# Last expert sums in the PSUM banks, norm weight as one row, and a square moved: a change to a hybrid decoder step with 32 experts

## The chip, the cores and the metric

One core of a Trainium2 chip. The metric is the device time of one launch in microseconds (us); the figure of the kernel before is the median of three runs. All data are f32.

## The reference

One decoder layer serves 256 prompt tokens (one sequence) and 8 sample tokens (eight sequences, one new token each) with the same weights, D = 1024. Adaptive norm, two recurrent mixers (HGRN2 and GLA), output projection and residual, a second norm, then a mixture of 32 experts of which each token takes 4, and a last norm. What matters here is the end:

```
h  = rms_norm(x, norm2_g) * (1 + sc2) + sh2
for each token, the sum over its 4 experts of
     gate * ( act(h @ w_up[e] + b_up[e]) @ w_down[e] + b_down[e] )
x  = x + g2 * that sum
y  = x * rsqrt(mean(x * x) + 1e-6) * final_norm_g
```

The weights are w_up (32, 1024, 2048) and w_down (32, 1024, 1024), 12 MB for an expert and 403 MB for all; every expert is read once.

## The kernel before, in words

The program is written for each engine by itself, with semaphores between them; nothing plans or reorders. SP issues the weight loads from HBM into SBUF as pieces of 2 MB (`pairs`, a ring of eight), in the order in which TensorE uses them, and waits before a piece until the one that had its place is used. A turn n of the expert loop (generator `experts`: four turns written out, hardware loops, four written out from `MIDDLE_AT` = 16 on, a loop, two written out) does on TensorE, in this order: gather of the tokens of expert n+1 by a one-hot product (line 1402), transposes of the up product (`back`, line 1449), `turn`, `combine` of expert n-1, first half of the up product of n+1 (`up`, line 1431), `gates` (line 1460), both halves of the down product of n (`down`, line 1486), and the second half of the up product. 64 slots serve an expert: 8 sample tokens and up to 56 prompt tokens; if an expert has more, an overflow loop at the end (`n_over > 0`) works through the rest.

`down` leaves the result of an expert as 128 partitions by 512: half 0 of the columns in partitions 0 to 63, half 1 in 64 to 127. VectorE multiplies it with g2 into `ysb` (`take_rows`, line 2097), and adds the sample rows to `acc_s` (line 2108). `combine` (line 1472) spreads `ysb` back to the tokens with the gates as the stationary operand: four products of 64 rows by 512 columns, for the blocks (0,0), (0,1), (1,0), (1,1) of the 256 x 1024 result (`COMBINE`), into four PSUM banks (`SUM_BANKS`, for the last two experts `LAST_BANKS` = 4, 7, 6, 0). VectorE adds the four banks to `acc` in SBUF (`add_up`, line 2092), which began as the residual x.

In turn 16, `biases` on TensorE and VectorE adds the experts' down biases of all tokens at once, and ends with two sets of sample rows (`rows`, line 1277) that ScalarE copies out of bank 4 (line 923, `take_sample_rows`): x and g2 of the samples. TensorE waits for both copies before it goes on with the gates.

At the end TensorE does: `back` of expert 31, down of 30 (two pieces of 16 instructions), down of 31 first half, combine of 30, down of 31 second half, combine of 31. Then the last norm:

- VectorE adds block by block (line 2092). ScalarE squares blocks 0, 1, 2 out of `acc` with an accumulator (line 962), VectorE the fourth (line 2202) and adds the partial sums (line 2206).
- ScalarE makes the reciprocal root (lines 968, 969). VectorE makes block (1,0) times weight (line 2208), ScalarE scales it (line 973); VectorE does the other three blocks in one instruction each (line 2212).
- The samples: GpSimd puts `ys` together (lines 661, 662, 664) and multiplies it with the weight (line 666); ScalarE squares it with an accumulator (line 971), TensorE adds the halves (line 1630), ScalarE takes root (lines 975, 976) and scales (line 978).
- SP writes four blocks of 256 KB (line 582) and two sample halves (line 585), each waiting for its own block, in the order (0,0), (0,1), (1,0), (1,1), samples.

The norm weight `fgrow`, the same row in all 128 partitions, and `fgs`, its halves in partitions 0 to 63 and 64 to 127, come by DMAs that repeat the row (lines 562 and 564), issued when the last up product is done.

Of the kernel before, what the change touches and what calls it, by code (L numbers as in the profile page):

```python
# [21 lines left out]
ALU = mybir.AluOpType  # L22
ACT = mybir.ActivationFunctionType
AX = mybir.AxisListType

P = 128
D = 1024
# [5 lines left out]
NE = 32  # L33
# [19 lines left out]
XE = 1  # L53
# [206 lines left out]
def build_step(nc, a, o):  # L260
    ctx = ExitStack()
    with ctx:
# [111 lines left out]
        fgrow = more[:, 0, :]  # L374
        fgs = more[:, 1, 0:512]
        bd = r_x[:, 512:1024]
        bdg = r_s[:, 1536:2048]
# [79 lines left out]
        def _(sp):  # L457
# [86 lines left out]
            for i in range(UPS):  # L544
                reuse(i)
                load(i, 0, "up", i)
            for e, e0, q in experts(sp):
                body(e, UPS + LOADS * e0, q)
            for e, kind, k in LAST[:-1]:
# [41 lines left out]
        def _(pool):  # L591
# [72 lines left out]
            od.link(g.tensor_tensor(ys, ys, junk_s, ALU.add), sem("ys_ready"))  # L664
            pool.wait_ge(sem("fg_in"), 48)
            od.did(g.tensor_tensor(yfs, ys, fgs, ALU.mult), sem("yfs_ready"))
# [3 lines left out]
        def _(act):  # L670
# [275 lines left out]
            with act.If(n_over > 0):  # L946
                with act.Fori(0, EXTRA) as j:
                    with act.If(j < n_over):
                        n = j + NE
                        take_gathered(n)  # L950
                        take_up(n)
                        take_gates(n)
                        glu_sigmoid(n, j * 2 + 2 * NE, n + 1)
                        act.nop()
                    act.nop()
                act.wait_ge(sem("acc_done"), 1)
# [27 lines left out]
        def _(pe):  # L984
# [477 lines left out]

            def combine(n, banks, xes, sampled=None, picks=None, gT=gpickT):

# [4 lines left out]
                for (i, half), b in zip(COMBINE, banks):  # L1469
                    if b == 6:  # L1470
                        pe.wait_ge(sem("xe_ready"), xes * XE)
                    mm(bank[:, b, :], gT[64 * half:64 * half + 64, P * i:P * i + P],  # L1472
                       ysb[64 * half:64 * half + 64, :], start=True, stop=True).then_inc(sem("acc_psum"), 1)

# [54 lines left out]
            def biases(n):  # L1529
# [80 lines left out]
            with pe.If(n_over > 0):  # L1610
                with pe.Fori(0, EXTRA) as j:
                    with pe.If(j < n_over):
# [11 lines left out]
                        pe.nop()  # L1624
                    pe.nop()
                pe.nop()

            pe.wait_ge(sem("pair_ready"), 4)
            pe.wait_ge(sem("squares_ready"), 4)
            mm(bank[:, 2, 0:1], pair[:, :], sumsq_s[:, :], start=True, stop=True).then_inc(sem("ssq_psum"), 1)  # L1630
# [3 lines left out]
        def _(dve):  # L1634
# [541 lines left out]
            with dve.If(n_over > 0):  # L2176
                with dve.Fori(0, EXTRA) as j:
                    with dve.If(j < n_over):
# [18 lines left out]
                    dve.nop()  # L2197
                v.memset(sumsq[:, 4:5], 0.0).then_inc(sem("acc_done"), 1)
                dve.nop()

            dve.wait_ge(sem("acc_used"), NA * NE)
            STT(ring[:, 15, 0:512], acc[1][:, 512:D], 1.0, acc[1][:, 512:D], ALU.mult, ALU.mult, accum_out=sumsq[:, 3:4]
                ).then_inc(sem("sums_ready"), 1)
            dve.wait_ge(sem("sums_ready"), 1)
            dve.wait_ge(sem("squares_ready"), 3)
            TT(sumsq[:, 5:7], sumsq[:, 0:4:2], sumsq[:, 1:4:2], ALU.add).then_inc(sem("sums_ready"), 1)
            dve.wait_ge(sem("fg_in"), 48)
            TT(ring[:, 13, 0:512], acc[1][:, 0:512], fgrow[:, 0:512], ALU.mult).then_inc(sem("yf1_ready"), 1)
            dve.wait_ge(sem("frstd_ready"), 1)
            for i, half in ((0, 0), (0, 1), (1, 1)):  # L2210
                own = slice(512 * half, 512 * half + 512)
                STT(ring[:, 12 + i, own], acc[i][:, own], sumsq[:, 5 + i:6 + i], fgrow[:, own], ALU.mult, ALU.mult
                    ).then_inc(sem("y0_ready"), 1)

# [67 lines left out]
```

## Time and profile before

| | us |
|---|---|
| median of 3 runs | 1158.92 (1158.68 to 1160.07) |
| the profiled execution, its own time | 1159.39 |
| its span, first to last instruction | 1157.6 |
| mean granted TensorE clock | 0.994 |
| TensorE (PE) busy | 1112.3 |
| VectorE (DVE) busy | 411.7 |
| ScalarE (ACT) busy | 191.3 |
| GpSimd (POOL) busy | 20.7 |
| read from HBM | 455.60 MB, 398 GB/s over the span |

PE is TensorE's matmuls and PEld its weight loads, which run beside them. A matmul of f32 shows as two instructions. SPq and the like are the sequencers' own work, such as issuing a DMA. An engine's busy time is no measure of what it costs: what counts is who waits for whom. The granted clock is a share of 2.4 GHz. Rows with "xN" merge N instructions that follow one another; the time beside them is from the first start to the last end.

### The profile page before, as it was taken

What the parts mean: (1) busy time and instruction counts of PE and PEld (TensorE: products, weight loads), DVE (VectorE), ACT (ScalarE), POOL (GpSimd) and SP (SyncE); (2) the same over time, 40 slices, a digit from 0 to 9 for tenths busy, and PEclk for the clock granted to TensorE, in tenths of its full rate; (3) what the DMA queues carried; (4) which work ended last, traced back from release to release, by engine and by line L of the source; (5) the groups of instructions that cost most, each with busy time, mean ns of one, the idle gap of its engine ahead of it and who ended that gap; (6) DMA issues with size and microseconds to landing.
All of it is one profiled execution on the core that took longest, in us unless ns stands there. A gap on an engine that the chain in (4) does not pass through costs nothing.

```text
span 1157.6 us, 14316 instructions
## 1 busy us (share of the span) xinstructions
PE 1112.3 (96%) x5674; PEld 497.2 (43%) x5674; DVE 411.7 (36%) x841; ACT 191.3 (17%) x387; POOL 20.7 (2%) x53
## 2 busy tenths in 40 slices
PE   7999999999999999999999998999999999999996
PEld 5777778843333333333333333333333333333332
DVE  3145644353333333333333334333333333333334
ACT  2161223321111111111111111111111111111112
POOL 0101010000000000000000000000000000000001
PEclk9999999999999999999999998999999999999998
DMA  9987986989999999999999999999999999999995
GB/s 352 411 308 257 367 274 231 415 316 400 429 412 430 429 426 427 429 428 428 429 429 429 429 429 427 428 427 427 427 430 425 428 428 429 428 429 428 428 429 199
DMA packets 43323, 460.96 MB, mean 398 GB/s; under 512 B 6965, under 2 KB 7937, under 8 KB 13673
## 3 DMA queue, kind: packets, MB, share of 16 engines
q1 hardware_dynamic: 37072, 449.66, 93.2%
q0 software_dynamic: 2688, 9.47, 2.3%
q10 hardware_dynamic: 3512, 1.14, 0.4%
q8 instruction: 34, 0.56, 0.2%
q14 instruction: 17, 0.13, 0.0%
HBM read 455.60 MB, written 4.65 MB: 398 GB/s over the span
## 4 chain that ended last, share of the span: by engine, by line
PE 73%; DMA 25%; DVE 1%; ACT 1%; issue 0%; SPq 0%; DVEq 0%; ACTq 0%
PE bank L1431 27%; DMA ring<-in_w_up 20%; PE bank L1486 14%; PE bank L1091 9%; PE bank L1472 5%; PE bank L1402 4%; DMA ring<-in_w_down 3%; PE bank L1314 2%; PE bank L1449 2%; DMA ring<-in_w_ada 2%; PE bank L1036 1%; PE bank L1411 1%; PE bank L1195 1%; PE bank L1460 1%; PE bank L1172 1%; PE bank L1277 1%
## 5 line engine op out<-in xcount | busy, mean ns | idle before, releaser
L1431 PE MATMUL bank<-ring,arena 128*64 128x512 f32 x2016 | 448.6, 595 | 21.2 <-DMA ring<-in_w_up 21.2
L1431 PEld LDWEIGHTS bank<-ring,arena 128*64 128x64 f32 x2016 | 139.7, 137 | 320.2 <-issue 277.0
L1486 PE MATMUL bank<-ring,arena 128*64 128x512 f32 x992 | 220.1, 595 | 1.9 <-DMA ring<-in_w_down 1.9
L1486 PEld LDWEIGHTS bank<-ring,arena 128*64 128x64 f32 x992 | 68.6, 137 | 131.8 <-issue 129.0
L1091 PE MATMUL bank<-arena,ring 128*128 128x264 f32 x448 | 105.4, 390 | 0.8 <-DVE arena L1696 0.8
L2043 DVE COPY arena<-bank 128x512 f32<-128x512 f32 x32 | 22.1, 692 | 197.9 <-PE bank L1431 197.9
L890 ACT ACTIVATE arena<-bank 128x512 f32<-128x512 f32 x32 | 19.1, 598 | 442.1 <-PE bank L1431 442.1
L1091 PEld LDWEIGHTS bank<-arena,ring 128*128 128x128 f32 x448 | 83.1, 190 | 17.9 <-issue 4.5
L2097 DVE TENSOR_TENSOR arena<-bank,arena 128x512 f32<-128x512 f32 x32 | 22.1, 692 | 189.7 <-PE bank L1486 189.7
L2092 DVE TENSOR_TENSOR arena<-arena,bank 128x512 f32<-128x512 f32 x128 | 79.1, 680 | 5.4 <-PE bank L1472 5.4
L1472 PE MATMUL bank<-arena,gpickT 64*128 64x512 f32 x248 | 78.6, 628 | 0.0
L2052 DVE TENSOR_TENSOR arena<-bank,bupT 128x512 f32<-128x512 f32 x64 | 43.9, 686 | 70.6 <-PE bank L1449 70.6
L1402 PE MATMUL bank<-arena,before 128*64 128x512 f32 x256 | 60.4, 592 | 0.0
L1975 DVE TENSOR_TENSOR arena<-before,arena 128x256 f32<-128x256 f32 x32 | 13.6, 425 | 119.4 <-PE bank L1460 119.3
L905 ACT ACTIVATE gpickT<-bank 128x256 f32<-128x256 f32 x31 | 11.9, 385 | 215.8 <-PE bank L1460 215.8
L1449 PEld LDWEIGHTS bank<-ident,arena 128*128 128x128 f32 x256 | 33.2, 209 | 25.0 <-issue 24.3
L1472 PEld LDWEIGHTS bank<-arena,gpickT 64*128 64x128 f32 x248 | 29.8, 185 | 27.6 <-issue 15.6
L1449 PE MATMUL bank<-ident,arena 128*128 128x128 f32 x256 | 39.1, 296 | 0.5 <-ACT arena L890 0.5
L1402 PEld LDWEIGHTS bank<-arena,before 128*64 128x64 f32 x256 | 18.3, 137 | 36.1 <-issue 36.0
L896 ACT ACTIVATE arena<-arena 128x512 f32<-128x512 f32 x32 | 20.1, 630 | 57.5 <-DVE arena L2057 57.5
L1314 PE MATMUL bank<-arena,ring 128*128 128x264 f32 x128 | 29.2, 388 | 0.0
L1314 PEld LDWEIGHTS bank<-arena,ring 128*128 128x128 f32 x128 | 24.1, 190 | 5.0 <-issue 1.1
(335 smaller groups left out, 688.4 us busy)
## 6 DMA issues: line engine op xcount, KB each, us to landing
ring<-in_w_up SPq DMA_DIRECT2D x125, 2048.0 KB, 29.1
ring<-in_w_down SPq DMA_DIRECT2D x61, 2048.0 KB, 28.1
ring<-in_w_ada SPq DMA_DIRECT2D x24, 1024.0 KB, 9.5
ring<-in_w_in SPq DMA_DIRECT2D x14, 1024.0 KB, 12.0
ring<-in_w_o SPq DMA_DIRECT2D x4, 1024.0 KB, 8.5
arena<-in_w_up SPq DMA_DIRECT2D x5, 512.0 KB, 18.8
arena<-in_w_down SPq DMA_DIRECT2D x5, 512.0 KB, 12.8
ring<-in_state_hgrn POOLq DMA_DIRECT2D x4, 512.0 KB, 13.3
```

Source lines behind the costliest of these rows:

```text
L896: act.activation(te, tg, ACT.Exp, scale=-ALPHA).then_inc(sem("glu_step"), 1)
L1091: last = mm(bank[:, proj_bank(n), 0:T], ring[:, slot, 512 * (k % 4) + P * i:512 * (k % 4) + P * i + P], hT[:, k, :], start=(k == 0), stop= ...
L1314: last = mm(bank[:, WO_BANK[m % 3], 0:T], ring[:, FRONT_SLOT[ld], c0:c0 + P], oT[:, k, :], start=(k == 0), stop=(k == KT - 1))
L1402: last = mm(bank[64 * half:64 * half + 64, 6, :], pick[:, i, :], h2tok[:, i, 512 * half:512 * half + 512], start=(i == 0), stop=(i == 1))
L1431: last = mm(bank[64 * half:64 * half + 64, b, :], xe[:, par, k % 4, k // 4, :], src[:, 512 * half:512 * half + 512], start=(k == 0), stop= ...
L1449: last = tr(bank[:, 2 + b, P * j:P * j + P], us[:, c0:c0 + 4 * P - 3:4], ident[:, :])
L1472: mm(bank[:, b, :], gT[64 * half:64 * half + 64, P * i:P * i + P], ysb[64 * half:64 * half + 64, :], start=True, stop=True).then_inc(sem(" ...
L1486: last = mm(bank[64 * half:64 * half + 64, b, :], acts[:, k, :], src[:, 512 * half:512 * half + 512], start=(k == 0), stop=(k == KT - 1))
L2043: v.tensor_copy(us[:, 512:1024], bank[:, 1, :]).then_inc(sem("us_dve"), 1)
L2052: return TT(dst.rearrange("p (j h s) -> p j h s", j=4, h=2), bank[:, 2 + b, :].rearrange("p (j h s) -> p j h s", j=4, h=2), bias(b).to_bro ...
L2092: TT(y, y, bank[:, b, :], ALU.add).then_inc(sem("acc_used"), 1)
L2097: TT(ysb, bank[:, b, :], g2h, ALU.mult).then_inc(sem("ysb_ready"), 1)
```

## The change

Six things change.

1. Before the first down product of expert 31, TensorE multiplies the identity with the four blocks of `acc`, into the four last banks, and leaves the sums open (`sums_to_banks(False)`).
2. The combines of experts 30 and 31 accumulate onto these banks (`start=False`). VectorE's eight adds of these experts go, and so does TensorE's wait for the adds of 30. If the overflow loop runs, VectorE first copies the banks back to `acc`, and TensorE puts the sums into the banks again at the end.
3. The last norm reads the banks in place of `acc`. ScalarE squares blocks 0, 2 and 3; VectorE copies block 1 to SBUF and squares it from there and from the bank.
4. The square of the samples goes from ScalarE to VectorE, ahead of the addition of the partial sums.
5. `final_norm_g` is loaded as one row into one partition, before the loads of turn 16; the three repeating DMAs at the end go.
6. In turn 16, after the sample rows, TensorE multiplies a row of ones with each half of this row, into banks 4 and 7, and ScalarE copies these into `fgrow` and `fgs`, two copies for each half; TensorE waits for all four.

```diff
@@ block.sync
             for e, e0, q in experts(sp):
+                if e0 == MIDDLE_AT:
+                    sp.wait_ge(sem("down_done"), 3)
+                    sp.dma_start(fgraw, a["final_norm_g"].unsqueeze(0)).then_inc(sem("fg_in"), 16)
                 body(e, UPS + LOADS * e0, q)
...
-            sp.wait_ge(sem("up_done"), NE)
-            sp.dma_start(fgrow, a["final_norm_g"].unsqueeze(0).to_broadcast([P, D])).then_inc(sem("fg_in"), 16)
-            for half in range(2):
-                sp.dma_start(fgs[64 * half:64 * half + 64, :], a["final_norm_g"][512 * half:512 * half + 512].unsqueeze(0)
-                             .to_broadcast([64, 512])).then_inc(sem("fg_in"), 16)
@@ block.scalar, take_sample_rows
+                for half in range(2):
+                    act.wait_ge(sem("bias_psum"), half + 6)
+                    own, b = slice(64 * half, 64 * half + 64), (4, 7)[half]
+                    act.activation(fgrow[:, 512 * half:512 * half + 512], bank[:, b, :], ACT.Copy).then_inc(sem("rows_sb"), 1)
+                    act.activation(fgs[own, :], bank[own, b, :], ACT.Copy).then_inc(sem("rows_sb"), 1)
@@ block.scalar, the end
-            def square(m):
-                i, half = COMBINE[m]
-                act.wait_ge(sem("acc_used"), NA * (NE - 1) + m + 1)
-                od.did(A(ring[:, 14, 512 * m:512 * m + 512], acc[i][:, 512 * half:512 * half + 512], ACT.Square,
+            for m in (0, 2, 3):
+                act.wait_ge(sem("acc_psum"), NA * (NE - 1) + m + 1)
+                od.did(A(ring[:, 14, 512 * m:512 * m + 512], bank[:, LAST_BANKS[m], :], ACT.Square,
                          accum_out=sumsq[:, m:m + 1]), sem("squares_ready"))
-            for m in range(3):
-                square(m)
-            act.wait_ge(sem("sums_ready"), 2)
+            act.wait_ge(sem("sums_ready"), 4)
             od.link(A(sumsq[:, 5:7], sumsq[:, 5:7], ACT.Ln, scale=1.0 / D, bias=eps_col[:, 0:1]))
             od.link(A(sumsq[:, 5:7], sumsq[:, 5:7], ACT.Exp, scale=-0.5), sem("frstd_ready"))
-            act.wait_ge(sem("ys_ready"), 1)
-            od.did(A(junk_s, ys, ACT.Square, accum_out=sumsq_s[:, 0:1]), sem("squares_ready"))
@@ block.tensor
+            def sums_to_banks(stop):
+                for m, ((i, half), b) in enumerate(zip(COMBINE, LAST_BANKS)):
+                    last = mm(bank[:, b, :], ident[:, :], acc[i][:, 512 * half:512 * half + 512], start=True, stop=stop)
+                    if stop:
+                        last.then_inc(sem("acc_done"), 1)
...
                 pe.wait_ge(sem("rows_sb"), 3)
+                pe.wait_ge(sem("fg_in"), 16)
+                for half in range(2):
+                    mm(bank[:, (4, 7)[half], :], ones[0:1, :], fgraw[:, 512 * half:512 * half + 512], start=True, stop=True
+                       ).then_inc(sem("bias_psum"), 1)
+                pe.wait_ge(sem("rows_sb"), 7)
...
             down(NE - 2, ld, rd)
             ld, rd = last_of(NE - 1, "down")
+            pe.wait_ge(sem("acc_used"), NA * (NE - 2))
+            pe.wait_ge(sem("gpick_sb"), NE)
+            pe.wait_ge(sem("xe_ready"), NE * XE)
+            sums_to_banks(False)
             down(NE - 1, ld, rd, (0,), 3, actT_last)
-            combine(NE - 2, LAST_BANKS, NE, None, NE)
+            combine(NE - 2, LAST_BANKS, NE, None, NE, start=False, stop=False)
             down(NE - 1, ld, rd, (1,), 3, actT_last)
-            pe.wait_ge(sem("acc_used"), NA * (NE - 1))
-            combine(NE - 1, LAST_BANKS, NE, None, NE, gpickT_last)
+            combine(NE - 1, LAST_BANKS, NE, None, NE, gpickT_last, start=False)
@@ block.vector
             take_rows(NE - 2)
-            add_up(NE - 2, LAST_BANKS)
+            dve.wait_ge(sem("acc_psum"), NA * (NE - 1))
             take_rows(NE - 1, sampled=False, b=3)
             STT(junk_s, bank[:, 3, :], gs[:, NE - 1:NE], g2s, ALU.mult, ALU.mult).then_inc(sem("acc_s_used"), 1)
-            add_up(NE - 1, LAST_BANKS)
...
-            dve.wait_ge(sem("acc_used"), NA * NE)
-            STT(ring[:, 15, 0:512], acc[1][:, 512:D], 1.0, acc[1][:, 512:D], ALU.mult, ALU.mult, accum_out=sumsq[:, 3:4]
-                ).then_inc(sem("sums_ready"), 1)
+            dve.wait_ge(sem("acc_psum"), NA * (NE - 1) + 2)
+            v.tensor_copy(ring[:, 15, 0:512], bank[:, LAST_BANKS[1], :]).then_inc(sem("sums_ready"), 1)
             dve.wait_ge(sem("sums_ready"), 1)
+            STT(ring[:, 15, 512:D], ring[:, 15, 0:512], 1.0, bank[:, LAST_BANKS[1], :], ALU.mult, ALU.mult,
+                accum_out=sumsq[:, 1:2]).then_inc(sem("sums_ready"), 1)
+            dve.wait_ge(sem("ys_ready"), 1)
+            STT(junk_s, ys, 1.0, ys, ALU.mult, ALU.mult, accum_out=sumsq_s[:, 0:1]).then_inc(sem("sums_ready"), 1)
+            dve.wait_ge(sem("sums_ready"), 2)
             dve.wait_ge(sem("squares_ready"), 3)
             TT(sumsq[:, 5:7], sumsq[:, 0:4:2], sumsq[:, 1:4:2], ALU.add).then_inc(sem("sums_ready"), 1)
-            dve.wait_ge(sem("fg_in"), 48)
-            TT(ring[:, 13, 0:512], acc[1][:, 0:512], fgrow[:, 0:512], ALU.mult).then_inc(sem("yf1_ready"), 1)
+            dve.wait_ge(sem("rows_sb"), 7)
+            TT(ring[:, 13, 0:512], bank[:, LAST_BANKS[2], :], fgrow[:, 0:512], ALU.mult).then_inc(sem("yf1_ready"), 1)
```

## Rows read from the trace of the kernel before

**Rows 1.** The page: DMA in 40 slices (tenths), and one group of instructions by line
```profile
DMA  9987986989999999999999999999999999999995
...
L2092 DVE TENSOR_TENSOR arena<-arena,bank 128x512 f32<-128x512 f32 x128 | 79.1, 680 | 5.4 <-PE bank L1472 5.4
```

**Rows 2.** The page: shares of the chain that ended last
```profile
PE 73%; DMA 25%; DVE 1%; ACT 1%; issue 0%; SPq 0%; DVEq 0%; ACTq 0%
```

**Rows 3.** Windows: busy PE, PEld, DVE, ACT, POOL, then PEclk, DMA share, GB/s
```profile
710.00:720.00 10.00, 7.65 (x42) 3.37 (x42) 2.15 (x4) 1.43 (x3) 0.00 (x0) 0.66 1.00 428
720.00:760.00 40.00, 40.00 (x188) 14.32 (x186) 11.05 (x20) 3.62 (x7) 0.00 (x0) 1.00 1.01 428
...
900.00:1000.00 100.00, 94.16 (x434) 34.12 (x430) 34.08 (x59) 12.90 (x22) 0.00 (x0) 1.00 1.01 428
```

**Rows 4.** Timeline, TensorE and VectorE from 1131 on: start, us, instruction [idle before]
```profile
1131.64 3.65 PE L1486 MATMUL bank<-ring,arena 128*64 128x512 f32 x16 [0.51 <-DMA ring<-in_w_down]
...
1136.65 3.65 PE L1486 MATMUL bank<-ring,arena 128*64 128x512 f32 x16 [1.36 <-DMA ring<-in_w_down]
...
1140.23 1.99 PE L1472 MATMUL bank<-arena,gpickT 64*128 64x512 f32 x8
...
1141.46 2.48 DVE L2092 TENSOR_TENSOR arena<-arena,bank 128x512 f32<-128x512 f32 x4 [4.77 <-PE bank L1472]
...
1142.15 3.65 PE L1486 MATMUL bank<-ring,arena 128*64 128x512 f32 x16
...
1145.85 0.69 DVE L2097 TENSOR_TENSOR arena<-bank,arena 128x512 f32<-128x512 f32 x1 [1.91 <-PE bank L1486]
...
1146.65 1.99 PE L1472 MATMUL bank<-arena 64*128 64x512 f32 x8 [0.84 <-issue]
```

**Rows 5.** Timeline, earlier TensorE products with a 128 by 128 tile
```profile
149.80 3.28 PE L1091 MATMUL bank<-arena,ring 128*128 128x264 f32 x14
...
188.86 1.98 PE L1113 MATMUL bank<-arena,ones 128*128 128x512 f32 x4
190.68 0.83 PE L1247 MATMUL bank<-ring 128*128 128x128 f32 x6
```

**Rows 6.** Timeline, what follows the last combination
```profile
1147.35 1.27 POOL L664 TENSOR_TENSOR arena<-arena 128x512 f32<-128x512 f32 x1 [7.90 <-DVE arena L2169]
...
1147.85 2.48 DVE L2092 TENSOR_TENSOR arena<-arena,bank 128x512 f32<-128x512 f32 x4 [0.65 <-PE bank L1472]
...
1148.70 1.27 POOL L666 TENSOR_TENSOR arena<-arena,more 128x512 f32<-128x512 f32 x1
...
1149.81 0.61 ACT L962 ACTIVATE ring<-arena 128x512 f32<-128x512 f32 x1
1150.33 0.19 ACT L962 ACTIVATION_READ_ACCUMULATOR ring<-arena 128x1 f32 x1
...
1151.10 0.16 DVE L2206 TENSOR_TENSOR sumsq<-sumsq 128x2 f32<-128x2 f32 x1
...
1151.94 2.08 DVE L2212 SCALAR_TENSOR_TENSOR ring<-arena,sumsq,more 128x512 f32<-128x512 f32 x3
...
1152.72 1.99 SPq L582 DMA_DIRECT2D out_yp<-ring  x4
...
1154.01 0.72 ACT L978 ACTIVATE arena<-arena,sumsq 128x512 f32<-128x512 f32 x1
1154.76 0.98 SPq L585 DMA_DIRECT2D out_ys<-arena  x2
```

**Rows 7.** The page: ScalarE's copy out of a bank
```profile
L890 ACT ACTIVATE arena<-bank 128x512 f32<-128x512 f32 x32 | 19.1, 598 | 442.1 <-PE bank L1431 442.1
```

**Rows 8.** Lines 562 and 564, the weight's DMAs, last rows of each answer
```profile
L564 SPq DMA_DIRECT2D more<-in_final_norm_g x2: 562/576/591, 1125.9 to 1126.5; - x2
...
DMA to landing us min/median/max: 16.0/16.8/17.6
```

**Rows 9.** Line 478, weight loads issued from 690 to 800
```profile
DMA to landing us min/median/max: 18.9/24.1/35.9
```

More of the change, by code:

```diff
@@ L375, in build_step @@
         fgs = more[:, 1, 0:512]
+        fgraw = more[0:1, 2, :]
         bd = r_x[:, 512:1024]
@@ L664, in _ @@
             od.link(g.tensor_tensor(ys, ys, junk_s, ALU.add), sem("ys_ready"))
-            pool.wait_ge(sem("fg_in"), 48)
+            pool.wait_ge(sem("rows_sb"), 7)
             od.did(g.tensor_tensor(yfs, ys, fgs, ALU.mult), sem("yfs_ready"))
@@ L955, in _ @@
                     act.nop()
-                act.wait_ge(sem("acc_done"), 1)
+                act.wait_ge(sem("acc_done"), 1 + NA)
                 act.nop()
-            def square(m):
-                i, half = COMBINE[m]
-                act.wait_ge(sem("acc_used"), NA * (NE - 1) + m + 1)
-                od.did(A(ring[:, 14, 512 * m:512 * m + 512], acc[i][:, 512 * half:512 * half + 512], ACT.Square,
+            for m in (0, 2, 3):
+                act.wait_ge(sem("acc_psum"), NA * (NE - 1) + m + 1)
+                od.did(A(ring[:, 14, 512 * m:512 * m + 512], bank[:, LAST_BANKS[m], :], ACT.Square,
                          accum_out=sumsq[:, m:m + 1]), sem("squares_ready"))
-            for m in range(3):
-                square(m)
-            act.wait_ge(sem("sums_ready"), 2)
+            act.wait_ge(sem("sums_ready"), 4)
             od.link(A(sumsq[:, 5:7], sumsq[:, 5:7], ACT.Ln, scale=1.0 / D, bias=eps_col[:, 0:1]))
             od.link(A(sumsq[:, 5:7], sumsq[:, 5:7], ACT.Exp, scale=-0.5), sem("frstd_ready"))
-            act.wait_ge(sem("ys_ready"), 1)
-            od.did(A(junk_s, ys, ACT.Square, accum_out=sumsq_s[:, 0:1]), sem("squares_ready"))
             act.wait_ge(sem("yf1_ready"), 1)
@@ L1461, in gates, with combine @@
                 last.then_inc(sem("gpick_psum"), 1)
-            def combine(n, banks, xes, sampled=None, picks=None, gT=gpickT):
+            def combine(n, banks, xes, sampled=None, picks=None, gT=gpickT, start=True, stop=True):
                 pe.wait_ge(sem("ysb_ready"), n + 1)
@@ L1472, in combine @@
                     mm(bank[:, b, :], gT[64 * half:64 * half + 64, P * i:P * i + P],
-                       ysb[64 * half:64 * half + 64, :], start=True, stop=True).then_inc(sem("acc_psum"), 1)
+                       ysb[64 * half:64 * half + 64, :], start=start, stop=stop).then_inc(sem("acc_psum"), 1)
+            def sums_to_banks(stop):
[3 more added lines that the diff above has]
+                        last.then_inc(sem("acc_done"), 1)
             def down(n, loads, rounds, pieces=range(DOWNS), b=5, acts=actT):
@@ L1625, in _ @@
                     pe.nop()
+                pe.wait_ge(sem("acc_done"), 1)
+                sums_to_banks(True)
                 pe.nop()
             pe.wait_ge(sem("pair_ready"), 4)
-            pe.wait_ge(sem("squares_ready"), 4)
+            pe.wait_ge(sem("sums_ready"), 3)
             mm(bank[:, 2, 0:1], pair[:, :], sumsq_s[:, :], start=True, stop=True).then_inc(sem("ssq_psum"), 1)
@@ L2176, in _ @@
             with dve.If(n_over > 0):
+                for m, ((i, half), b) in enumerate(zip(COMBINE, LAST_BANKS)):
+                    dve.wait_ge(sem("acc_psum"), NA * (NE - 1) + m + 1)
+                    for part in range(2):
+                        c0 = 256 * part
+                        v.tensor_copy(acc[i][:, 512 * half + c0:512 * half + c0 + 256], bank[:, b, c0:c0 + 256]
+                                      ).then_inc(sem("acc_used"), 1)
                 with dve.Fori(0, EXTRA) as j:
@@ L2198, in _ @@
                 v.memset(sumsq[:, 4:5], 0.0).then_inc(sem("acc_done"), 1)
+                dve.wait_ge(sem("acc_done"), 1 + NA)
                 dve.nop()
-            dve.wait_ge(sem("acc_used"), NA * NE)
-            STT(ring[:, 15, 0:512], acc[1][:, 512:D], 1.0, acc[1][:, 512:D], ALU.mult, ALU.mult, accum_out=sumsq[:, 3:4]
-                ).then_inc(sem("sums_ready"), 1)
+            dve.wait_ge(sem("acc_psum"), NA * (NE - 1) + 2)
+            v.tensor_copy(ring[:, 15, 0:512], bank[:, LAST_BANKS[1], :]).then_inc(sem("sums_ready"), 1)
             dve.wait_ge(sem("sums_ready"), 1)
+            STT(ring[:, 15, 512:D], ring[:, 15, 0:512], 1.0, bank[:, LAST_BANKS[1], :], ALU.mult, ALU.mult,
[3 more added lines that the diff above has]
+            dve.wait_ge(sem("sums_ready"), 2)
             dve.wait_ge(sem("squares_ready"), 3)
             TT(sumsq[:, 5:7], sumsq[:, 0:4:2], sumsq[:, 1:4:2], ALU.add).then_inc(sem("sums_ready"), 1)
-            dve.wait_ge(sem("fg_in"), 48)
-            TT(ring[:, 13, 0:512], acc[1][:, 0:512], fgrow[:, 0:512], ALU.mult).then_inc(sem("yf1_ready"), 1)
+            dve.wait_ge(sem("rows_sb"), 7)
+            TT(ring[:, 13, 0:512], bank[:, LAST_BANKS[2], :], fgrow[:, 0:512], ALU.mult).then_inc(sem("yf1_ready"), 1)
             dve.wait_ge(sem("frstd_ready"), 1)
@@ L2211, in _ @@
                 own = slice(512 * half, 512 * half + 512)
-                STT(ring[:, 12 + i, own], acc[i][:, own], sumsq[:, 5 + i:6 + i], fgrow[:, own], ALU.mult, ALU.mult
-                    ).then_inc(sem("y0_ready"), 1)
+                STT(ring[:, 12 + i, own], bank[:, LAST_BANKS[COMBINE.index((i, half))], :], sumsq[:, 5 + i:6 + i], fgrow[:, own],
+                    ALU.mult, ALU.mult).then_inc(sem("y0_ready"), 1)
 def ada_blocks(w):
```

## The prediction

> **What bounds the kernel now.** I read the page first: the DMA engines are full from the tenth of the 40 slices to the last but one, at half in the last [rows 1]. The chain that ended last gives TensorE 73% and DMA 25% [rows 2]. The reader is to see that these two take turns: a stage of 100 us has TensorE busy for 94 with the DMA share at 1.01 and 428 GB/s [rows 3]. So the transfer of 2 MB pieces is the floor of the long middle, and what TensorE does there costs only if it drains the queue. At the end it turns round. The timeline of the last 27 us [rows 4] shows TensorE waiting twice for weights, once 0.51 us before the second half of the down weights of expert 30 (1131.64) and once 1.36 us before the first half of those of expert 31 (1136.65). From there on it runs without a wait for DMA: 16 instructions of the down product, the combination of expert 30 (1140.23), 16 more (1142.15), and then the last combination at 1146.65, which waits for VectorE's product with g2 (1145.85). Call that start T. Everything behind T is a chain of vector operations: four adds, squares, reciprocal root, products, and six output DMAs that SP issues one behind another [rows 6]. The run ends 10.95 us after T, at 1157.6. So this change is judged by two things: how far T moves, and how long the chain behind T is.
>
> The profiled execution took 1159.39 us with its span of 1157.6, so 1.79 us lie around it; it is 0.47 us above the median of 1158.92. I sum on the span and add the difference to the median.
>
> **The identity products, TensorE.** Four products of a 128x128 identity with a 128x512 block of acc, each two instructions as every f32 product here: 8 instructions. They sit between the last down product of expert 30 and the first of expert 31. What they wait for is long done: VectorE works in order and has the adds of expert 29 behind it before it even starts the gated product of expert 31, and the copied gates belong to the turn before. The nearest rows for the price: the same tile and width, line 1113, puts four instructions in 188.86 to 190.68, 0.455 each; line 1091, the same tile with 264 columns, has 14 starts in 3.28 us, so (3.28 - 0.39) / 13 = 0.222 each, by 512/264 that is 0.431 [rows 5]. Eight cost 3.45 us (0.431) to 3.64 us (0.455); I take 3.45, since the second row has more instructions in a stream. The 16 instructions from 1131.64 make room after 3.58 us, as those from 1136.65 do (next group at 1140.23), so at 1135.22. The identity products then end at 1138.67 and the down product of expert 31 starts there, instead of 1136.65: the weight wait of 1.36 us covers part, 2.02 us are left over. If nothing hid it, it would be 3.45. What is late next is TensorE itself, for 3.58 + 1.92 + 3.65 us up to T. That the combinations now accumulate costs nothing: the down products accumulate already at the same pace (16 instructions in 3.58 us). The wait for the adds of expert 30 before the last combination goes; those adds ended at 1143.94 [rows 4], 2.7 us before T, so it held nobody. T moves to 1148.67, by +2.02 (bounds +1.9 to +2.25).
>
> **Behind T, ScalarE and VectorE.** Before, the first add starts at T+1.20, three more follow at 0.6 each, the sum of the last block comes at T+3.71, its read at T+4.33, the small addition (line 2206) at T+4.45 [rows 6]. The change takes out the four adds (2.48 us) and reads the banks. Banks 4 and 7 are there at T+1.20; banks 6 and 0 with the end of the eight matmuls, T+1.99. ScalarE: square of block 0 at T+1.20; block 2 waits for its bank, T+2.05; block 3 follows after 0.61, and its accumulator is read 0.52 + 0.19 later: T+3.37. That its source is a bank should not cost: a ScalarE copy out of a bank takes 598 ns, the square from SBUF 0.61 us [rows 6, 7]. VectorE: copy of bank 7 at T+1.20, 0.69 (an add from a bank is 680 ns [rows 1]); square at T+1.93; then the sample square, which waits for ys, ready when GpSimd's add ends (T+0.70+1.27 = T+1.97), so no wait: start T+1.93+0.70 = T+2.63, accumulator read at T+3.25 to T+3.33. The small addition then starts at T+3.42, when both are through, instead of T+4.45: 1.03 us earlier. As bounds I take 0.9 and 1.1: by 0.05 each the two squares may be longer than the rows that I use, and the small addition may come 0.07 earlier if the order of the semaphores is kinder.
>
> From there the order is as before: logarithm, exponent (0.84 us to the first final product), first product 0.75, first output DMA 0.78 after its start: T+5.04. The six issues take 3.02 us back to back (1152.72 to 1155.74 [rows 6]), and up to the end of the span there are 1.86 more. Does something arrive later than its issue? Block (1,0): its product on VectorE T+3.50, scaled by ScalarE T+4.25 to T+4.96, issue at T+6.0, no. Last final product T+4.26+2.08 = T+6.34, issue T+6.5, no, though by little. Samples: TensorE's sum over the halves is out by T+4.1 at a pair of instructions, ScalarE comes to it behind the (1,0) scaling at T+4.96, makes the root in at most the 0.84 of the other one and scales in 0.72: ready T+6.5, issue T+7.08. Before, the samples' scaling (1154.73) and SP's free slot (1154.76) came together, so moving the sample square to VectorE removes a second wait that would otherwise hold at T+8.1. The final products now take 0.69 from one start to the next and the adds out of banks 0.6 [rows 6], so a bank as their source adds nothing that I can see; 0.05 each would not reach SP, but for the first. The end moves by +2.02 - 1.03 = +1.0 us.
>
> **The norm weight.** Removed: the three repeating DMAs. The later two were issued at 1125.9 and 1126.5 and landed 16.0 to 17.6 us later, by 1144.1, before T and long before anyone multiplies with the weight [rows 8]. Together they moved 0.77 MB (128 rows of 4 KB and 128 of 2 KB) at the end of the queue; no output is under way then. Gain 0 to 0.5: should they have been mixed with the weights of expert 30, this would be 1.8 us of the stream, but TensorE is ready at 1131.64 - 0.51 = 1131.13 and only its 0.51 us of wait can go. I take 0, because the next piece comes 5.0 us later (1131.64 to 1136.65), the 4.9 us that 2.1 MB need at 428 GB/s and no more. Added: one row of 4 KB before the loads of expert 16's turn. SP's wait there is for the third down product, which is hundreds of us old; it is issued with loads that lie eight pieces, 39 us, ahead of TensorE, and the longest landing of that stretch is 35.9 us [rows 9], while TensorE asks for it only at the end of its bias stage, about 720. In the middle, behind the sample rows, two products of one row by 512 columns, four instructions, 1.7 us at full clock, and four ScalarE copies of 0.60 [rows 7] that follow from the first: 1.0 + 2.4 + 0.2 = 3.6 us by which TensorE falls back, 4.6 at half clock. In this stage TensorE waits on other engines several times already, busy 7.65 of 10 us with a granted clock of 0.66, yet the DMA share stays 1.00 [rows 3]. The pieces issued in 690 to 800 landed in 18.9 us at least, against 35.9 at most [rows 9]: the stage eats some 17 us of the queue's lead. 3.6 more leave over 15, where a piece alone needs 4.9. Cost 0; without that cover 3.6 to 4.6.
>
> The overflow loop does not run: 128 adds for 32 experts [rows 1], so its new instructions are only jumped over, VectorE's branch in the time between its product with g2 and T+1.20.
>
> **Sum:** +2.02 - 1.03 + 0 + 0 = +1.0 us: span 1158.6, profiled 1160.4, median 1159.9. A change of 0.2%, about 2.3 us here, is what can be told from none; this is less than half.
>
> **Rivals.**
> *Port (24%).* The sample square is new on VectorE, with both inputs in SBUF, and GpSimd multiplies ys with the weight at the same time: ready at T+2.05, 1.27 long, to T+3.32. In the rows of before no such pair overlaps: GpSimd's instructions run beside adds with one input in a bank (2.48 us for four, as always), and its last one ends at 1149.97, before VectorE's square of the last block [rows 6]. If VectorE's square has to wait until GpSimd is through, it starts at T+3.35 instead of T+2.63, and the small addition goes to T+4.1: 0.7 later. Then +1.7: 1160.6. Against it: no row; for it: none either. The Trainium skill states just this in SBUF — State Buffer, section Who interferes with whom: a VectorE instruction with two SBUF inputs contends with a GpSimd instruction that reads SBUF, through the shared read interface, and the pair is an exclusive lock. By that rule the time would be the 1160.6; no row of before can show it.
>
> *The tail's weights come earlier (12%).* The broadcasts slowed them: TensorE goes on at 1131.13, -0.5: 1159.4. For it speaks that all three were issued while the weights of experts 30 and 31 were under way in the same queue [rows 4, 8]; against it the steady distance of the pieces.
>
> *The middle is not hidden (5%), slower.* The place is expert 16's turn. If the standing lasts so long that the clock stays at half through the following down and up products (7.0 us each at full clock, twice that then), the lag grows by 4.6 + 7.0 + 7.0 = 18.6, while only 18.9 - 4.9 = 14.0 of lead are there; from there each us of lag is lost. That costs 4.6 us: 1164.5. It decides when the DMA share between 715 and 760 falls below 1. Against it: behind the present stall the clock is 1.00 again in the whole of 720 to 760 [rows 3].
>
> *The identity products hide wholly (5%).* TensorE has no second gap there; it would need their cost under 1.4 us, against 3.4 by two rows. Then only the gain stays: 1157.9.
>
> *My forecast (45%)*, and the rest (9%) for shifts of a us either way that no part explains; the three runs of before lie 1.4 us apart. Range 1158.2 to 1161.6: it takes in the forecast, port and earlier weights with the bounds of their terms, and leaves out the middle and the fully hidden case. Faster than 1156.6 is 5% (shifts on top of full hiding or of earlier weights), slower than 1161.2 is 12% (the middle 5, the upper ends of port and of the shifts 7), within 83%.
>
> **What would show it.** Eight identity matmuls from about 1135.2, 3.4 us, and no DMA wait before the down product of expert 31, which starts near 1138.7. The last combination at 1148.7. The small addition 3.4 us behind it (4.1 if the port rules), the first output DMA 5.0 behind. In the middle, DMA share 1.0 throughout and TensorE again waiting for weights before 900. I am wrong if T moves by less than 1.5 or more than 2.5, or if the span between T and the end does not shrink by 0.3 to 1.1.

## The result, and the profile after

The changed kernel takes 1161.53 us (median of 20 runs, 1159.99 to 1164.28), the kernel before in the same 20 rounds 1159.34 (1158.49 to 1161.24). The ratio is 1.0019, 95% interval 1.0013 to 1.0025: slower by 2.2 us, inside the 0.2% that I had called "no change", but twice the +1.0 us of my sum. The interval leaves out 1, so the loss is real, though small. The profiled execution has a span of 1159.5 us (1157.6 before).

The timeline of TensorE at the end of the changed kernel (start, us, instruction); line 1491 is `down`, 1476 the identity products, 1470 `combine`:

```profile
1127.65 7.21 PE L1491 MATMUL bank<-ring,arena 128*64 128x512 f32 x32
...
1134.80 3.70 PE L1476 MATMUL bank<-arena,ident 128*128 128x512 f32 x8
...
1138.43 3.65 PE L1491 MATMUL bank<-ring,arena 128*64 128x512 f32 x16
...
1142.01 1.99 PE L1470 MATMUL bank<-arena,gpickT 64*128 64x512 f32 x8
...
1143.93 3.65 PE L1491 MATMUL bank<-ring,arena 128*64 128x512 f32 x16
...
1148.45 1.99 PE L1470 MATMUL bank<-arena 64*128 64x512 f32 x8 [0.86 <-DVE arena L2112]
```

Against [rows 4]: eight instructions from 1134.80 to 1138.43, 3.63 us, and no wait for weights before expert 31's down product. T, the start of the last combination, is at 1148.45 instead of 1146.65.

Behind T, the timeline of VectorE, GpSimd, ScalarE and SP of the changed kernel, which answers to [rows 6]:

```profile
1149.61 0.60 ACT L965 ACTIVATE ring<-bank 128x512 f32<-128x512 f32 x1 [18.71 <-PE bank L1470]
1149.65 0.69 DVE L2222 COPY ring<-bank 128x512 f32<-128x512 f32 x1 [0.60 <-PE bank L1470]
...
1150.54 1.27 POOL L664 TENSOR_TENSOR arena<-arena,more 128x512 f32<-128x512 f32 x1
...
1150.98 1.36 DVE L2227 SCALAR_TENSOR_TENSOR arena<-arena 128x512 f32<-128x512 f32 x1
...
1151.53 0.20 ACT L965 ACTIVATION_READ_ACCUMULATOR ring<-bank 128x1 f32 x1
...
1152.28 0.15 DVE L2230 TENSOR_TENSOR sumsq<-sumsq 128x2 f32<-128x2 f32 x1
...
1153.11 2.07 DVE L2236 SCALAR_TENSOR_TENSOR ring<-bank,sumsq,more 128x512 f32<-128x512 f32 x3
...
1153.89 2.28 SPq L580 DMA_DIRECT2D out_yp<-ring  x4
...
1156.21 1.54 SPq L583 DMA_DIRECT2D out_ys<-arena  x2
```

Two things are to be seen. The sample square (line 2227) takes 1.36 us, while GpSimd's product with the weight (line 664) runs until 1151.81; the small addition waits for it and starts 0.55 us after ScalarE's last read has ended (1151.73). And the outputs: six issues take 3.86 us instead of 3.02, and from the first issue to the end there are 5.61 us instead of 4.88.

### The profile page after: what moved, and what is told of

Same layout as the page of the kernel before. It is cut to its first block, busy times and chain, and to the rows that moved or that the text cites. A ratio compares the mean times of both kernels' runs of the same rounds, so it can differ in the third digit from the quotient of the medians.

```text
span 1159.5 us, 14336 instructions
## 1 busy us (share of the span) xinstructions
PE 1119.1 (97%) x5686; PEld 500.0 (43%) x5686; DVE 408.5 (35%) x836; ACT 192.8 (17%) x389; POOL 20.6 (2%) x53
## 4 chain that ended last, share of the span: by engine, by line
PE 82%; DMA 16%; DVE 1%; ACT 1%; issue 0%; ACTq 0%; DVEq 0%; SPq 0%
PE bank L1429 31%; PE bank L1491 17%; DMA ring<-in_w_up 15%; PE bank L1089 9%; PE bank L1470 6%; PE bank L1400 4%; PE bank L1447 3%; PE bank L1312 2%; PE bank L1034 1%; PE bank L1409 1%; PE bank L1193 1%; PE bank L1458 1%; PE bank L1015 1%; DMA ring<-in_gn_gla 1%; PE bank L1170 1%; PE bank L1275 1%
## 5 line engine op out<-in xcount | busy, mean ns | idle before, releaser
L2107 DVE TENSOR_TENSOR arena<-arena,bank 128x512 f32<-128x512 f32 x120 | 74.2, 679 | 0.0
```

The source lines that it names most:

```text
L2107: TT(y, y, bank[:, b, :], ALU.add).then_inc(sem("acc_used"), 1)
```

## The experiments

All traces were read at the same points. The table's distances are in us; "first issue to end" runs from the first output DMA's issue to the end of the span, and the last column says when the last transfer of instruction code (queue 14 of the DMA view) starts, in steps of 0.2 us. T here is absolute and moves with the time at which the weights come, so the columns behind it are distances.

| kernel | T | T to small addition | T to first output issue | six issues | first issue to end | last code transfer, from first issue |
|---|---|---|---|---|---|---|
| before | 1146.65 | 4.45 | 6.07 | 3.02 | 4.88 | +0.2 |
| before, second trace | 1146.83 | 4.45 | 6.07 | 3.02 | 4.90 | +0.2 |
| e9, before with code never run | 1147.40 | 4.45 | 6.07 | 3.11 | 4.93 | +0.4 |
| e1, norm weight alone | 1147.31 | 4.45 | 6.07 | 3.15 | 4.92 | +0.4 |
| changed | 1148.45 | 3.83 | 5.44 | 3.86 | 5.61 | +0.8 |
| changed, second trace (e6) | 1148.29 | 3.84 | 5.45 | 3.86 | 5.56 | +0.8 |
| e10, without the code never run | 1148.42 | 3.85 | 5.46 | 3.87 | 5.62 | +0.8 |
| e2, new end, old norm weight | 1150.23 | 3.85 | 5.45 | 3.15 | 5.62 | +0.8 |
| e4, no identity products | 1146.43 | 3.84 | 5.45 | 3.54 | 5.32 | +0.8 |
| e3, GpSimd held back | 1148.14 | 3.39 | 5.01 | 3.03 | 5.35 | +3.0 |
| e8, identity products early | 1151.32 | 3.38 | 5.00 | 3.02 | 5.48 | +3.0 |
| e5, sample square on ScalarE | 1149.20 | 3.39 | 5.01 | 2.97 | 5.49 | +1.8 |
| e7, hybrid | 1147.20 | 4.34 | 5.96 | 3.03 | 5.74 | +3.8 |
| e11, hybrid, second version | 1147.40 | 3.58 | 5.20 | 3.03 | 5.50 | +3.2 |

**e1, the norm weight alone** (kernel before, with parts 5 and 6 of the change):

```diff
+                    sp.dma_start(fgraw, a["final_norm_g"].unsqueeze(0)).then_inc(sem("fg_in"), 16)
...
+                pe.wait_ge(sem("rows_sb"), 7)
```

> Only the weight of the last norm is changed (one row, spread by TensorE in turn 16); the end is that of before. Theory A (all of the loss lies in the tail: identity products, port, output issues): the time of before, ratio 1.000, DMA share 1.0 through 700 to 760, last combination at the same distance behind the last weight wait as before. Rival B (the middle stage costs about 1.2 us that the sum left out): ratio 1.001.

Ratio 1.0002 (0.9993 to 1.0011): the middle is hidden. The windows of the changed kernel say how (busy PE, PEld, DVE, ACT, POOL, PEclk, DMA share, GB/s), against [rows 3]:

```profile
710.00:720.00 10.00, 7.75 (x40) 3.29 (x38) 2.06 (x4) 1.15 (x2) 0.00 (x0) 0.66 1.02 433
720.00:730.00 10.00, 8.60 (x24) 2.77 (x26) 0.72 (x2) 2.69 (x6) 0.00 (x0) 0.66 1.01 429
730.00:760.00 30.00, 30.00 (x144) 10.89 (x140) 9.21 (x16) 3.47 (x6) 0.00 (x0) 1.00 1.01 427
```

and the landing of the weight loads issued from 690 to 800 in it, against [rows 9]:

```profile
DMA to landing us min/median/max: 12.6/17.3/35.4
```

The granted clock is 0.66 in 720 to 730 too (1.00 before), the DMA share never falls, and the shortest landing goes from 18.9 to 12.6 us. My 3.6 to 4.6 us of lag were 6.3, still covered, since one piece alone needs 4.9.

**e2, the new end alone** (the changed kernel with the three repeating DMAs of before):

```diff
+            sp.dma_start(fgrow, a["final_norm_g"].unsqueeze(0).to_broadcast([P, D])).then_inc(sem("fg_in"), 16)
```

> The opposite: the new end with the three repeating DMAs of before. Theory A: the time of the changed kernel, ratio 1.0019 to before. Rival B: 1.0009. If the repeating DMAs had delayed the last weights (rival of the prediction), TensorE waits for the second half of expert 30's down weights again by some 0.5 us, here as before, and it does not in the changed kernel.

Ratio 1.0020 (1.0012 to 1.0029), as the changed kernel. So the whole loss lies in the end. TensorE waited 0.51 us for the second down piece of expert 30 here, and not in the changed kernel; but the second trace of before has no such wait either, and there the three DMAs are in place. And the trace of e10 has a wait of 0.42 us at this place without the three DMAs. It comes and goes from one execution to the next. The rival of the weights that come earlier is not borne out.

**e4, no identity products** (the residual and the sums of experts 0 to 29 are left out):

```diff
-            sums_to_banks(False)
...
-            combine(NE - 2, LAST_BANKS, NE, None, NE, start=False, stop=False)
+            combine(NE - 2, LAST_BANKS, NE, None, NE, start=True, stop=False)
```

> The changed kernel without the identity products: the residual and the sums of experts 0 to 29 are left out of the result. Theory A: TensorE waits for expert 31's down weights again (about 1.4 us), the last combination comes 1.8 to 2.2 us earlier, the time falls by as much, to about 1159.5, ratio 1.0002 or a little under 1. Rival (the products are hidden by the wait for weights): no change, ratio 1.0019.

Ratio 1.0001 (0.9992 to 1.0010), against 1.0019: the identity products cost some 2.1 us, known to about 1.2 us by the two intervals. The timeline of TensorE says where:

```profile
1127.82 7.23 PE L1491 MATMUL bank<-ring,arena 128*64 128x512 f32 x32
...
1136.41 3.65 PE L1491 MATMUL bank<-ring,arena 128*64 128x512 f32 x16 [1.36 <-DMA ring<-in_w_down]
...
1146.43 1.99 PE L1470 MATMUL bank<-arena 64*128 64x512 f32 x8 [0.86 <-DVE arena L2111]
```

From the start of expert 30's down product to T it is 18.61 us, in the changed kernel 1148.45 - 1127.65 = 20.80: 2.19 more, which is 3.63 us of products less the wait of 1.36 and a little. The cost depends on the execution that one compares with. In both traces of the kernel before it is 19.17 us from there to T, with 1.87 and 1.95 us of waits for weights in them, and against these the products cost 1.63. Over the five traces without identity products (before twice, e1, e4, e9) the two waits before the down products add up to between 1.34 and 2.54 us. What should have been a gain of the new end, with the identity products taken away, still leaves nothing: the small addition is 0.61 us earlier than before, and 0.4 of it go in the outputs.

**e3, GpSimd held back:**

```diff
             pool.wait_ge(sem("rows_sb"), 7)
+            pool.wait_ge(sem("sums_ready"), 3)
             od.did(g.tensor_tensor(yfs, ys, fgs, ALU.mult), sem("yfs_ready"))
```

> The changed kernel, with GpSimd's product of ys with the weight made to wait until VectorE's sample square is done. Port theory: the sample square falls from 1.36 to 0.69 us, and the small addition comes 3.4 us behind the start of the last combination instead of 3.8; time 0.4 us less than the changed kernel. Rival (the square is long for another reason, such as both operands being one tensor): it stays 1.36 us.

The timeline of this kernel:

```profile
1150.68 0.69 DVE L2228 SCALAR_TENSOR_TENSOR arena<-arena 128x512 f32<-128x512 f32 x1
...
1151.53 0.16 DVE L2231 TENSOR_TENSOR sumsq<-sumsq 128x2 f32<-128x2 f32 x1 [0.15 <-ACT ring L966]
1151.55 1.28 POOL L665 TENSOR_TENSOR arena<-arena,more 128x512 f32<-128x512 f32 x1 [1.39 <-DVE arena L2228]
```

The same instruction, both operands still one tensor, takes 0.69 us when GpSimd is silent, and the small addition comes at T+3.39, now held by ScalarE. So it is shown that the two instructions slow VectorE's down when they run together, and that the operands being one tensor is not the reason. That it is the read interface which they share, and not for instance that both read `ys`, was not separated. Time 1161.08, ratio 1.0015 (1.0006 to 1.0023): the direction is right, the 0.4 us are below what the runs resolve.

**e5, the sample square back on ScalarE:**

```diff
-            STT(junk_s, ys, 1.0, ys, ALU.mult, ALU.mult, accum_out=sumsq_s[:, 0:1]).then_inc(sem("sums_ready"), 1)
...
+            od.did(A(junk_s, ys, ACT.Square, accum_out=sumsq_s[:, 0:1]), sem("squares_ready"))
```

> The changed kernel with the sample square back on ScalarE, behind the reciprocal root. No VectorE instruction with two SBUF inputs runs beside GpSimd any more: the small addition at 3.4 us behind the last combination's start (3.83 in the changed kernel), first output DMA at 5.0 (5.44). The scaled samples come at about 7.1 and so as late as SP's free slot. If the outputs take longer in the changed kernel because of the new order around the samples (first issue to end 5.6 us there, 4.9 before), they go back to 4.9 here and the ratio to before is 1.0007; if the slower outputs have another cause, they stay above 5.3 and the ratio is 1.0012.

Small addition at 3.39, issues back to back in 2.97, as expected; but first issue to end 5.49 and ratio 1.0017 (1.0008 to 1.0025). So part 4 of the change is worth nothing here, and the longer outputs are not its doing.

**e6, the changed kernel again** (no edit).

> The changed kernel once more, for a second trace of its end. If the stretch from the first output DMA to the end (5.61 us in its first trace, 4.88 before) belongs to the kernel, it is above 5.3 again; if it is scatter from one execution to another, it may be anywhere from 4.9 to 5.6. The last combination starts 1.8 us later than in before against the weights' arrival, the small addition 3.83 behind it.

Ratio 1.0016 (1.0007 to 1.0024), 5.56 us from the first issue to the end, the same 3.86 us of issues. The longer outputs come again in a second execution, so they are the kernel's own and not scatter.

**e7 and e8, other places for the identity products.** e8 puts all four between the two down pieces of expert 30, with GpSimd held back; e7 does so with blocks 0 and 2 only, leaves blocks 1 and 3 to VectorE's adds, and has the sample square on ScalarE:

```diff
+            down(NE - 2, ld, rd, (0,))
             pe.wait_ge(sem("acc_used"), NA * (NE - 2))
...
             sums_to_banks(False)
+            down(NE - 2, ld, rd, (1,))
```

> Identity products for blocks 0 and 2 alone, placed between the two down pieces of expert 30; blocks 1 and 3 added by VectorE as before; sample square on ScalarE; GpSimd's product with the weight waits for VectorE's square. If the cost of the identity products is what the waits for weights (0.5 + 1.4 us) don't cover, the two (1.8 us) cost nothing, while the small addition comes at 3.5 instead of 4.45 us: 0.9 us faster than before, ratio 0.9992. If the outputs lengthen in every version that reads banks, the gain is 0.3 or less, ratio 0.9997 or more.

> All four identity products, but placed between the two down pieces of expert 30, so that both waits for weights cover them, and GpSimd's product held back as in e3. Expected: last combination 1.3 us later than in before instead of 1.8, small addition at 3.4: 0.3 us slower than before by this sum (ratio 1.0003), 0.5 to 0.8 more if the outputs take longer again. If the second wait alone counts, it is as e3 (1.0015).

Both miss. e8: ratio 1.0017 (1.0007 to 1.0027), and 20.67 us from expert 30's down product to T against 20.80. Neither trace has a wait for weights in this stretch: the products had used up both waits wherever they stood, so moving them gains nothing. e7: 1.0012 (1.0003 to 1.0020). Its small addition is at T+4.34, for VectorE stood still in front of its square (timeline of e7):

```profile
1148.44 1.47 DVE L2198 TENSOR_TENSOR arena<-arena,bank 128x512 f32<-128x512 f32 x2 [0.69 <-PE bank L1476]
...
1150.80 0.69 DVE L2247 SCALAR_TENSOR_TENSOR ring<-arena 128x512 f32<-128x512 f32 x1 [0.89 <-DVE arena L2198]
```

Behind the two adds stand only the load of the overflow count, the branch, and the square. The load and what follows it on VectorE's sequencer, by its source line in e7:

```profile
L2209 DVEq TENSOR_LOAD <-table x1: 546/546/546, 1149.2 to 1149.2; - x1
L2209 DVEq FUSED_REGOPS  x1: 223/223/223, 1149.8 to 1149.8; - x1
```

The load starts at 1149.2, as the last add does (the two adds end at 1149.91), and the register work ends at 1150.0; the branch and the square at 1150.80 come behind it. In the kernel before it starts at 1148.7, with two of the four adds still to come, and none of this shows.

**e11, the second hybrid:** the load of the count ahead of the adds, and nothing added in the overflow block.

```diff
+            n_over = dve.value_load(table[0:1, EXTRA:EXTRA + 1], min_val=0, max_val=EXTRA)
             dve.wait_ge(sem("acc_used"), NA * (NE - 2) + 2)
             add_odd(NE - 1)
-            n_over = dve.value_load(table[0:1, EXTRA:EXTRA + 1], min_val=0, max_val=EXTRA)
```

> The hybrid of e7 without the added code in the overflow block, and with VectorE's load of the overflow count ahead of its last adds (in e7 VectorE stood still 0.89 us behind them, before its square). Expected: small addition at 3.5 to 3.9 behind the last combination's start (4.34 in e7), first output at 5.1 to 5.5; with an output stretch of 4.9 that is 0.5 to 0.9 us faster than before, ratio 0.9993; with 5.5 it is equal to before.

The standstill is gone (small addition at 3.58). The two edits were not run apart, but the trace speaks for the load: it now starts at 1146.7, before the last adds. The time is 1159.44 us, ratio 0.9996 (0.9987 to 1.0005). That is the best of these kernels, 2.2 us under e10 in the same rounds, and not to be told from the kernel before. Its two identity products cost nothing: it has no wait for weights, and 18.99 us from expert 30's down product to T (19.17 before). Of the 0.87 us by which its small addition comes earlier than before, the outputs take back 0.62.

**e9 and e10, the longer outputs: code that never runs.** e9 is the kernel before with four products and eight copies inside the overflow block; e10 the changed kernel without what it added there:

```diff
+                    mm(bank[:, b, :], ident[:, :], acc[i][:, 512 * half:512 * half + 512], start=True, stop=True
...
-                        v.tensor_copy(acc[i][:, 512 * half + c0:512 * half + c0 + 256], bank[:, b, c0:c0 + 256]
```

> The kernel before, and nothing more than instructions inside the overflow block that is jumped over (four identity products for TensorE, eight copies for VectorE, about as much as the change adds there). Theory C (the outputs take longer because the added code that never runs shifts when the last code is fetched): the stretch from the first output DMA to the end grows from 4.9 to 5.3 or more, ratio 1.0004. Rival (the longer stretch comes from what the new end executes): 4.9, ratio 1.0000.

> The changed kernel without what it adds inside the overflow block (the copies of the banks to acc, the second identity products); these inputs never enter it. Theory C: first output DMA to end back at 4.9, ratio 1.0012. Rival: 5.6 as in both traces of the changed kernel, ratio 1.0018.

e9: 4.93 us, ratio 1.0002 (0.9993 to 1.0011). e10: 5.62 us, ratio 1.0014 (1.0005 to 1.0023). This theory falls: it is not the added code that isn't run.

**e12, the kernel before again** (no edit).

> The kernel before once more, for a second trace of its end and as a control of the ratio: last combination to small addition 4.45, first output DMA to end 4.9, ratio 1.0000. If the stretch comes out at 5.3 or more, it is scatter and no property of the new end.

4.45, 3.02 and 4.90 us, ratio 0.9998 (0.9989 to 1.0007).

What does sort the fourteen traces is the last column of the table: when the last transfer of instruction code (queue 14) runs, in steps of 0.2 us. The DMA view of the 0.2 us from 0.2 behind the first issue, kernel before:

```profile
DMA packets 1, 0.01 MB, mean 41 GB/s; under 512 B 0, under 2 KB 0, under 8 KB 0
## 3 DMA queue, kind: packets, MB, share of 16 engines
q14 instruction: 1, 0.01, 12.8%
```

and from 0.8 behind the first issue, changed kernel:

```profile
DMA packets 24, 0.06 MB, mean 276 GB/s; under 512 B 0, under 2 KB 0, under 8 KB 23
## 3 DMA queue, kind: packets, MB, share of 16 engines
q1 hardware_dynamic: 23, 0.05, 62.1%
q14 instruction: 1, 0.01, 22.9%
```

In the four traces with the old end the code is under way alone, before the first output packet (which comes at about +0.8); in the ten with a new end it is among the output packets. The transfer rates show the effect, windows of the kernel before and then of the changed one (last two columns: DMA share, GB/s):

```profile
1155.92:1156.32 0.40, 0.00 (x0) 0.00 (x0) 0.00 (x0) 0.00 (x0) 0.00 (x0) 0.50 0.99 358
1156.32:1156.72 0.40, 0.00 (x0) 0.00 (x0) 0.00 (x0) 0.00 (x0) 0.00 (x0) 0.50 0.46 108
1156.72:1157.12 0.40, 0.00 (x0) 0.00 (x0) 0.00 (x0) 0.00 (x0) 0.00 (x0) 0.50 0.00 0
```

```profile
1157.49:1157.89 0.40, 0.00 (x0) 0.00 (x0) 0.00 (x0) 0.00 (x0) 0.00 (x0) 0.50 0.52 128
1157.89:1158.29 0.40, 0.00 (x0) 0.00 (x0) 0.00 (x0) 0.00 (x0) 0.00 (x0) 0.50 0.22 46
1158.29:1158.69 0.40, 0.00 (x0) 0.00 (x0) 0.00 (x0) 0.00 (x0) 0.00 (x0) 0.50 0.10 26
```

Before, the last packets end at 4.0 us behind the first issue; in the changed kernel some straggle until 4.7.

Two more readings speak for the code transfer. The first is how the outputs end where the issues are as short as before. In e11 the code starts at +3.2 and takes 15.8% of 16 engines over 0.2 us, 0.51 us on one engine. The windows of e11 that start 4.1 and 4.5 us behind the first issue:

```profile
1156.68:1157.08 0.40, 0.00 (x0) 0.00 (x0) 0.00 (x0) 0.00 (x0) 0.00 (x0) 0.50 0.07 26
1157.08:1157.48 0.40, 0.00 (x0) 0.00 (x0) 0.00 (x0) 0.00 (x0) 0.00 (x0) 0.50 0.02 5
```

A share of 0.07 is about one of the 16 engines: the others are through when they are in the kernel before, and one works on for some 0.6 us, about what the code took on one engine. The second is the third issue. In the changed kernel the code takes 22.9% of 16 engines over 0.2 us, so 0.73 us, and the third output issue takes 0.74 us (SP's timeline):

```profile
1154.93 0.74 SPq L580 DMA_DIRECT2D out_yp<-ring  x1
```

Before, it takes 0.45. In all five traces with a long third issue (changed, e6, e10, e2 and e4) it ends 0.13 to 0.15 us after the code transfer has ended. Still, the code transfer was not moved by itself (it would take a kernel that only moves it), so this cause is argued from the times and not shown. What decides when the code is fetched stays open; the split between old and new ends is without exception.

## Why the prediction was right, and where its sum was not

The forecast was slower by less than can be told from none. The kernel is slower, by 0.19%, and its 1161.53 us lie 0.07 us inside the upper end of the range, in the part above 1161.2 to which I had given 12%. That it still lies inside is in part luck: a term of 0.7 us that stood in no rival was covered by room left for others. One of my own signs of being wrong came true: the span between T and the end should have shrunk by 0.3 to 1.1 us, and it went from 10.95 to 11.05. By its steps:

- Identity products: T was to move by +2.02 (1.9 to 2.25). Between the profiled executions of before and changed it moved by 1.80, between e4 and the changed kernel by 2.02, and counted from expert 30's down product by 1.63 and 2.19. They took 3.63 us, the price of the 0.455 row, which has just their tile and width; I had taken 3.45 from the narrower one. The mechanism is right (products less the wait for weights that they fill), but the wait is not the constant of 1.36 that I subtracted, so the bounds were too narrow.
- Accumulating combinations, VectorE's adds gone, TensorE's wait gone: no cost, 3.65 and 1.99 us as before. Right.
- The chain from T to the small addition: -1.03 forecast, -0.62 measured. With GpSimd held back it is 3.39 against my 3.42, so each duration was right and the meeting with GpSimd is the whole difference. This is the rival that I gave 24%: the step "so no wait: start T+1.93+0.70 = T+2.63" held for the start (1150.98 is T+2.53), but not for the 0.70 us. I had put its price at 0.7; it is 0.44, because the small addition would have had to wait for ScalarE until T+3.4 anyway. The Trainium skill (SBUF — State Buffer, Who interferes with whom) says that such a pair contends, and e3 agrees. Its word of an exclusive lock is not quite what the row looks like: GpSimd takes 1.27 us as always, and VectorE is done 0.53 us after it, less than its own 0.69.
- Outputs: "The six issues take 3.02 us back to back ..., and up to the end of the span there are 1.86 more." This is the step that failed. Both were copied from the trace of before as constants. They are 5.61 instead of 4.88 together: +0.73, no part of my sum and of no rival. It took back more than the 0.62 us gained behind T.
- Norm weight: 0 forecast, 1.0002 measured. Right, though the lag was 6.3 us and not 3.6 to 4.6, and the clock stayed low longer. One sign did not come: the changed kernel has no wait for weights between 800 and 900, where before has three, and the first comes after 900. It costs nothing, for the DMA share stays at 1.

The sum of the profiled executions is +1.80 - 0.62 + 0.73 = +1.9 us, the difference of their spans; the medians of 20 runs say +2.2. Against the forecast of +1.0, the outputs miss by 0.7 and the meeting with GpSimd by 0.4, and T came 0.2 earlier than forecast in this pair of traces. The other rivals fell: DMA share 1.0 in the middle, and no sign of earlier weights.

## What to carry to other kernels

Moving adds from VectorE to TensorE pays only if TensorE has the room, and the room here was the wait for weights, 1.3 to 2.5 us from one execution to another, for 3.6 us of work in f32. Half of the work (e11) fitted in. When a square or product with both inputs in SBUF is put on VectorE, look at what GpSimd does at that moment. And the last stretch, from the first output issue to the end, is not a constant of the kernel: take it from several traces, and give it a range (4.9 to 5.7 us here) rather than carry it over to 0.01.

## What the runs showed of the hardware

- VectorE, square of 128x512 f32 out of SBUF, both inputs there: 0.69 us alone, 1.36 and 1.37 beside a GpSimd product of 1.27 us, which itself was not slowed (1.27 us in the kernel before too).
- An f32 product of the full 128 by 128 tile over 512 columns takes 0.91 us here (3.63 for four).
- SP's issue of one 256 KB output took 0.34 to 0.74 us, that of a 16 KB output 0.39 to 0.97 (kernel before and changed kernel).
- One transfer of instruction code runs near the end in every trace, at +0.2 to +3.8 us from the first output issue, and where it lay among the output packets the outputs took 5.3 to 5.7 us instead of 4.9.
- The load of a count into a register of VectorE took 0.55 us and the register work behind it 0.22 us. In the kernel before it ran beside the adds and cost nothing; in e7, behind the last two adds, it stood in a standstill of 0.89 us.
